# A hybrid attention and convolution block: mixer weights split in block 0 only, stored and loaded back, with layernorms on VectorE

## The reference

```
h   = LN0(concat(meta, x))
q, k, v, cb, cc, ch, gates = split(h @ w_in)          # 512,128,128,512,512,512,2048
y_attn = window_attention(q, k, v, sinks) @ w_attn_out # chunks of 64, own + previous + meta, ALiBi, sink
y_conv = (cb * conv3(cc * ch)) @ w_conv_out            # causal, 3 taps, depthwise
g_a, g_c = sigmoid(gates)
h = LN1(alpha * h + (g_a * y_attn + g_c * y_conv) @ w_o)
h = LN2(alpha * h + hierarchical_moe(h))               # 4 groups x 8 experts, top 2
```

## Time and profile before

| | |
|---|---|
| median of three runs | 4327.14 us |
| the profiled execution, its own time | 4333.28 us |
| its span, first to last instruction | 4331.5 us |
| mean granted TensorE clock | 0.988 |
| PE, weight load, DVE, ScalarE, POOL busy | 4171, 3429, 2519, 1773, 1095 us |
| DMA moved | 601 MB, mean 139 GB/s |

### The profile page before, as it was taken

One profiled execution on the slowest core, in us unless ns is written; L12 is line 12 of the kernel. 1 busy time (PEld: TensorE's weight loads), 2 busy tenths in 40 slices (PEclk: granted clock), 3 DMA queues, 4 the chain that ended last, 5 costly groups with the idle time before them and its releaser, 6 DMA issues. The chain is left out here.

```text
span 4331.5 us, 62892 instructions
## 1 busy us (share of the span) xinstructions
PE 4171.0 (96%) x20252; PEld 3428.8 (79%) x20253; DVE 2518.7 (58%) x3263; ACT 1773.0 (41%) x2950; POOL 1094.6 (25%) x1117
## 2 busy tenths in 40 slices
PE   7999999999999999999999999499999999999997
PEld 7887887887887888888888887388788888778886
DVE  5555555555555655645645645777666666765664
ACT  2422422422422422422422422466555555654553
POOL 4022032022022021121121121134333333333333
PEclk9999999999999999999999999799999999999998
DMA  6333333333333333333332332187666666765562
GB/s 171 85 107 103 93 102 98 99 104 97 102 104 89 107 106 85 107 104 89 111 102 80 117 102 78 54 289 248 246 199 198 206 199 234 251 203 198 194 204 90
DMA packets 569472, 601.49 MB, mean 139 GB/s; under 512 B 104080, under 2 KB 426640, under 8 KB 569248
## 3 DMA queue, kind: packets, MB, share of 16 engines
q1 hardware_dynamic: 521152, 476.88, 35.5%
q0 software_dynamic: 48096, 121.71, 8.4%
HBM read 527.15 MB, written 124.78 MB: 151 GB/s over the span
## 5 line engine op out<-in xcount | busy, mean ns | idle before, releaser
L826 PE MATMUL bank<-hT_hi,w_hi 128*128 128x512 f32 x2176 | 864.8, 397 | 30.1 <-DVE w_lo L658 21.3
L658 DVE TENSOR_TENSOR w_lo<-raw,w_hi 128x1024 fp32r<-128x1024 f32 x400 | 597.3, 1493 | 485.5 <-ACT w_hi L517 484.4
L827 PE MATMUL bank<-hT_lo,w_hi 128*128 128x512 f32 x2176 | 850.6, 391 | 2.4 <-issue 2.4
L828 PE MATMUL bank<-hT_hi,w_lo 128*128 128x512 f32 x2176 | 849.2, 390 | 0.0
L1565 PE MATMUL e_bank<-e_w_hi,e_xT_hi 128*128 128x512 f32 x1312 | 521.9, 398 | 14.2 <-DVE e_xT_lo L1488 12.4
L826 PEld LDWEIGHTS bank<-hT_hi,w_hi 128*128 128x128 f32 x2176 | 408.9, 188 | 140.4 <-DVE w_lo L658 32.6
L1567 PE MATMUL e_bank<-e_w_hi,e_xT_lo 128*128 128x512 f32 x1312 | 514.3, 392 | 0.0
L1566 PE MATMUL e_bank<-e_w_lo,e_xT_hi 128*128 128x512 f32 x1312 | 513.4, 391 | 0.0
L1493 DVE TENSOR_TENSOR e_w_lo<-e_raw,e_w_hi 128x1024 fp32r<-128x1024 f32 x384 | 444.4, 1219 | 117.7 <-ACT e_w_hi L1441 110.8
L828 PEld LDWEIGHTS bank<-hT_hi,w_lo 128*128 128x128 f32 x2176 | 408.9, 188 | 87.4
L827 PEld LDWEIGHTS bank<-hT_lo,w_hi 128*128 128x128 f32 x2176 | 409.3, 188 | 86.6 <-issue 5.4
(11 more groups left out here) (277 smaller groups left out, 7173.3 us busy)
## 6 DMA issues: line engine op xcount, KB each, us to landing
raw<-in_w_in_dram SPq DMA_DIRECT2D x251, 512.0 KB, 3.9
e_raw<-in_w_exp_gate_dram SPq DMA_DIRECT2D x128, 512.0 KB
e_raw<-in_w_exp_up_dram SPq DMA_DIRECT2D x128, 512.0 KB
e_raw<-in_w_exp_down_dram SPq DMA_DIRECT2D x128, 512.0 KB
h_rows<-h_rows SPq DMA_DIRECT2D x72, 512.0 KB, 3.5
raw<-in_w_o_dram SPq DMA_DIRECT2D x64, 512.0 KB, 3.8
raw<-in_w_in_dram SPq DMA_DIRECT2D x64, 256.0 KB, 3.7
raw<-in_w_attn_out_dram SPq DMA_DIRECT2D x64, 256.0 KB, 2.8
```

What stands on the lines that cost most here:

```text
L658: v.tensor_tensor(w_lo[:, s % 2, :], raw[:, s % RAW, :], w_hi[:, s % 2, :].bitcast(FP32), ALU.subtract).then_inc(lo_ready, 1)
L826: pe.matmul(out, hi, x_hi, start=first, stop=False)
L827: pe.matmul(out, hi, x_lo, start=False, stop=False)
L828: return pe.matmul(out, lo, x_hi, start=False, stop=last)
```

## The change

- **The split is done once.** Block 0 is written out ahead of the loops (`block_of_strips(0, True)`), and only there are strips loaded raw (3 buffers) and split, now two strips ahead. SP stores each split strip, hi and lo together, 1 MB, to a DRAM tensor `split_weights`. The loops run over blocks 1 to 7 and load the stored 1 MB into one of four slots: SP waits until strip s is finished on PE (`hold(sp, strip_done, ...)`), then loads strip s+3. PE waits for the load (`w_in`), ScalarE and DVE have no split there.
- **x loads** stand at MIX0 + 3 + i and no longer at MIX0 + 8 + i in SP's order.
- **Loop ends**: the loops of PE, ScalarE and DVE are written with a hint for the branch back; those of SP and POOL are as before.
- **Attention** and the v transposes go by ATT0 = CONV0 + 1, one strip later.
- **Layernorms**: DVE does both passes, subtract and gain, then scale and bias; POOL keeps the reciprocal deviation.
- DVE waits for its own mT_lo of the strip before, ahead of overwriting work[2], and the branch on block 0 for bias_prev becomes straight code.

The diff, cut to its core:

```diff
-    RAW = 5
-    assert N % RAW == 0 and N % 2 == 0
+    RAW, META_RAW = 3, 5
+    SLOTS = 4
+    ahead = RAW
+    slot_of = list(range(SLOTS)) * 5 + [0, 1, 2] + list(range(SLOTS)) * 6 + [0, 1, 2]
+    def first_slot(s):
+        return (s + 1) % RAW
     CONV0 = 2 + PAIRS
+    ATT0 = CONV0 + 1
...
-        raw = sb("raw", [P, RAW, D])
-        w_hi = sb("w_hi", [P, 2, D], F32R)
-        w_lo = sb("w_lo", [P, 2, D], F32R)
+        split_d = nc.dram_tensor("split_weights", [N, P, 2 * D], FP32).ap()
...
+        slots = [place(at, f"w_slot{i}", [P, 2, D], F32R) for i in range(SLOTS)]
+        raw = place([weights + 4 * 6 * D], "raw", [P, RAW, D])
...
-        X_AT = {MIX0 + 8 + i: i for i in range(TILES)}
+        X_AT = {MIX0 + 3 + i: i for i in range(TILES)}
...
             def _(sp):
-                def load(s, b):
-                    hold(sp, lo_ready, b * N + s + 1)
-                    for dst, src in strip_dmas(*strips[s % N], raw[:, s % RAW, :]):
+                def load_raw(s):
+                    if s >= RAW:
+                        sp.wait_ge(lo_ready, s - RAW + 1)
+                    for dst, src in strip_dmas(*strips[s], raw[:, s % RAW, :]):
                         sp.dma_start(dst, src).then_inc(raw_in[s % RAW], 16)
+                def store_split(s):
+                    sp.wait_ge(lo_ready, s + 1)
+                    sp.dma_start(split_d[s], slots[first_slot(s)][:, :, :].rearrange("p h d -> p (h d)").bitcast(FP32))\
+                      .then_inc(w_out[first_slot(s)], 16)
+                def load_split(s, b):
+                    sp.wait_ge(w_out[first_slot(s)], 16 * (sum(first_slot(q) == first_slot(s) for q in range(s + 1))))
+                    sp.dma_start(slots[slot_of[s]][:, :, :].rearrange("p h d -> p (h d)").bitcast(FP32), split_d[s])\
+                      .then_inc(w_in[slot_of[s]], 16)
+                def block_of_loads(b, first):
                     for s in range(N):
-                        load(s + 1, b)
+                        if first:
+                            store_split(s)
+                        if first and s + ahead < N:
+                            load_raw(s + ahead)
+                        else:
+                            hold(sp, strip_done, b * N + s + 3)
...
+                            load_split((s + ahead) % N, b + (s + ahead) // N)
...
             def _(po):
...
-                        scale(b * LNS + i1 - 1, i1 - 1, h, g1, b1)
-                    scale(b * LNS + TILES - 1, TILES - 1, h, g1, b1)
...
             def _(a):
-                def split_hi(b, s):
-                    uses = raw_uses(s, b) if s < N else raw_uses(0, b + 1)
-                    a.wait_ge(raw_in[s % RAW], uses)
-                    a.wait_ge(strip_done, b * N + s + 1)
-                    a.activation(w_hi[:, s % 2, :], raw[:, s % RAW, :], ACT.Copy).then_inc(hi_ready, 1)
+                def split_hi(s):
+                    a.wait_ge(raw_in[s % RAW], raw_uses(s))
+                    if s >= RAW:
+                        a.wait_ge(strip_done, s - RAW + 3)
+                        a.wait_ge(w_out[first_slot(s)], 16 * (sum(first_slot(q) == first_slot(s) for q in range(s))))
+                    a.activation(slots[first_slot(s)][:, 0, :], raw[:, s % RAW, :], ACT.Copy).then_inc(hi_ready, 1)
...
-                        split_hi(b, s + 1)
+                        if first and s + 2 < N:
+                            split_hi(s + 2)
...
+                block_of_strips(0, True)
+                with nc.Fori(1, BLOCKS, engines=bass.OrderedEngineSet([a.engine]), hint_back_edge=True) as b:
+                    block_of_strips(b, False)
...
             def _(v):
...
-                    v.tensor_scalar(rows[:, i1, :], rows[:, i1, :], moments[:, i1, 0:1], rstd[:, i1, 0:1],
-                                    ALU.subtract, ALU.mult).then_inc(ln_normed, 1)
+                    gain, shift = (g1, b1) if rows is h else (g0, b0)
+                    v.scalar_tensor_tensor(out=rows[:, i1, :], in0=rows[:, i1, :], scalar=moments[:, i1, 0:1],
+                                           in1=gain[:, :], op0=ALU.subtract, op1=ALU.mult).then_inc(ln_normed, 1)
+                    v.wait_ge(ln_normed, n + 1)
+                    v.scalar_tensor_tensor(out=rows[:, i1, :], in0=rows[:, i1, :], scalar=rstd[:, i1, 0:1],
+                                           in1=shift[:, :], op0=ALU.mult, op1=ALU.add).then_inc(ln_done, 1)
...
-                        split_lo(s + 1)
+                        if first and s + 2 < N:
+                            split_lo(s + 2)
...
             def _(pe):
...
-                        n = s - CONV0
-                        if s == CONV0:
-                            taken = out_no[(s - 1, 0)]
+                        n = s - ATT0
+                        if s == ATT0:
+                            taken = out_no[(CONV0 - 1, 0)]
...
-                        pe.wait_ge(lo_ready, b * N + RAW + s + 1)
+                        if first:
+                            pe.wait_ge(lo_ready, s + 1)
+                            w_of = slots[first_slot(s)]
+                        else:
+                            pe.wait_ge(w_in[slot_of[s]], w_uses(s, b))
+                            w_of = slots[slot_of[s]]
```

More of the change, by code:

```diff
@@ L245, in _ @@
                 sp.dma_start(xs[:, :, :], x[0:TOK, :].rearrange("(t p) d -> p t d", p=P)).then_inc(x_in, 16)
-                for n in range(1, RAW):
+                for n in range(1, META_RAW):
                     load_strip(n)
@@ L402, in mixer @@
         h1_out = [sem(f"h1_out{i}") for i in range(TILES)]
+        w_in = [sem(f"w_in{i}") for i in range(SLOTS)]
+        w_out = [sem(f"w_out{i}") for i in range(RAW)]
         hi_ready = sem("hi_ready")
@@ L439, in mixer, with raw_uses, w_uses @@
         LNS = 2 * TILES
[L441 to L446, removed]
+        def raw_uses(s):
+            return sum(16 * len(strip_dmas(*strips[q], raw[:, 0, :])) for q in range(s % RAW, s + 1, RAW))
+        def w_uses(s, b):
+            slot = slot_of[s]
+            return 16 * ((b - 1) * slot_of.count(slot) + slot_of[0:s + 1].count(slot))
         with nc.Block() as block:
@@ L473, in _ @@
                             sp.dma_start(xs[:, i1, :], x[bass.ds(nxt * TOK + i1 * P, P), :]).then_inc(x_in[i1], 16)
+                for s in range(ahead):
+                    load_raw(s)
+                block_of_loads(0, True)
+                with sp.Fori(1, BLOCKS) as b:
+                    block_of_loads(b, False)
+                for s in range(ahead):
+                    sp.wait_ge(w_in[slot_of[s]], w_uses(s, BLOCKS))
                 for i1 in range(TILES):
@@ L643, in _, with split_lo, block_of_strips @@
                 v.sem_inc(hx_lo, 1)
[L644 to L647 removed]
+                def split_lo(s):
+                    slot = slots[first_slot(s)]
+                    v.wait_ge(hi_ready, s + 1)
+                    v.tensor_tensor(slot[:, 1, :], raw[:, s % RAW, :], slot[:, 0, :].bitcast(FP32),
+                                    ALU.subtract).then_inc(lo_ready, 1)
+                def block_of_strips(b, first):
                     steps = [0]
@@ L724, in _ @@
                              .then_inc(s_prep, 1)
-                            if n == 1:
-                                with v.If(b == 0):
-                                    v.tensor_copy(bias[0:CHUNK, :, META:PREV], bias_prev[:, :, :])\
-                                     .then_inc(prev_set, 1)
+                            if n == 1 and first:
+                                v.tensor_copy(bias[0:CHUNK, :, META:PREV], bias_prev[:, :, :]).then_inc(prev_set, 1)
                                 v.wait_ge(prev_set, 1)
@@ L802, in _ @@
                     assert steps[0] == DVE_STEPS
+                for s in range(2):
+                    split_lo(s)
+                block_of_strips(0, True)
+                with nc.Fori(1, BLOCKS, engines=bass.OrderedEngineSet([v.engine]), hint_back_edge=True) as b:
+                    block_of_strips(b, False)
                 v.wait_ge(wo_taken, BLOCKS * 2 * TILES + 1)
```

72 lines of the change are left out of this document (34 added, 38 removed).

## The result

The changed kernel takes 4297.57 us (median of 7 runs, 4289.16 to 4307.51) against 4331.25 us for the kernel before (7 runs, 4320.51 to 4341.16). The ratio is 0.9923, 95% interval 0.9905 to 0.9941: 33.7 us faster by the medians. The forecast was 4295 and 32 us. Its profiled execution took 4303.45 us, with a span of 4301.6; the one of the kernel before took 4333.28.

What follows compares the result with a forecast made beforehand. TensorE, busy 96% of the span, was taken as the bound, so only its waits could pay. Waits of 25.5 us plus loop ends of 7, less 1 for block 0, about 32, took 4327.1 to 4295 us; range 4285 to 4305.

Steps and rivals of the forecast that it cites:

- What bounds: Whole kernel: TensorE busy 96% of the span, so only its waits, all in strips 0 to 7 of a block, can pay.
- The split leaves: 1.21 + 1.28 us a block: PE's waits for VectorE's split before strip 5 (1.21 us) and behind the second scores in strip 7 (1.28 us) go.
- Attention later: 0.69: At the v transposes behind the last q strip, PE's 0.69 us wait for ScalarE's q copy goes in each block.
- Loop ends: 1.0, bounds 0.4 to 1.4: At block starts, stops for issue behind the branch shrink: 1.0 us each, 7 us over 7 ends, bounds 3 to 10.
- strip 1's part: At a block's start, PE's 0.56 us wait for the late split of strip 1 goes, even if the hint does nothing.
- Layernorms at nothing, cover named: VectorE pays 10 to 13 us a block more, hidden before the router (strip 18) and strip 41; uncovered, at most 13.
- Loads, 0 to 3 us a block: Stored 1 MB loads land in 6.5 us of 10.9, slack 4.4; h1 stores in strips 4 to 7 fit; cost 0.
- Block 0: Raw loads plus 1 MB stores fit at DMA share 0.84: cost 0, bounds 0 to 40 us; 1 us deducted for attention.
- A: Strips with h1 stores in seven loop blocks: queue waits replace the split's, 4313 to 4322 us, no change; 14%.
- B: Strips 4 to 8 of loop blocks, and block 0: queue too slow at 230 GB/s, 4366 to 4405 us, slower; 10%.
- D: Loop blocks: PE's split waits become equally long waits for weights; only q copy and loop ends won, 4315 us; 4%.
- C: Product pitch falls 1 ns or small waits inside attention go: 10 to 15 us more gain, 4280 to 4285 us; 14%.

Runs made afterwards that it cites:

- w_only: Kernel before with only the stored weights and their x loads: 4312.3 us, ratio 0.9949, block period 325.1 against 328.4.
- a_att_early: Changed kernel with v transposes and attention back at their earlier strip: block period 323.5 against 322.6, 4312.4 us in one execution.
- b_hint: Kernel before with only the hint on the loops of PE, ScalarE and VectorE: block period 326.6 against 328.4, 4334.2 us in one execution.
- a_pool_ln: Changed kernel with the layernorms' gain and bias passes back on POOL: block period 322.6, unchanged; 4304.1 us in one execution.
- b_ln: Kernel before with only the layernorms changed, both passes on VectorE: block period 331.6 against 328.4, 4357.5 us in one execution.
- a_extra: Changed kernel with one more unused 512 KB load a strip in blocks 1 to 7: block period 322.6, unchanged; 4293.6 us in one execution.
- a_ahead2: Changed kernel with stored weights loaded for strip s+2 and not s+3: block period 325.8 against 322.6, 4333.7 us in one execution.
- b_all: Kernel before with later attention, VectorE layernorms and hint, weights still split in every block: 4367.3 us, ratio 1.0081.
- b_att: Kernel before with only attention and v transposes one strip later: block period 331.3 against 328.4, 4356.4 us in one execution.

## Why the prediction was right, point by point

- **What bounds.** Right in the main. Nothing in the mixing strips moved (144.9 us from strip 18 to strip 42 before, 144.95 after), and of the 5.8 us by which the period fell all but some 0.7 come from the places named in strips 0 to 7. The rest came from strips 5 to 14, in pieces too small to be in the list of waits.
- **The split leaves: 1.21 + 1.28 us a block.** Shown by w_only: 1.21 and 1.35, and 0.5 more in strips 5, 13 and 14. The whole period fell by 3.3.
- **Attention later: 0.69.** It was 0.95 (a_att_early). The bracket is idle time against a modelled end; from start to start it was 1.08 - 0.23 = 0.85, and I should have used that, as I did for strip 5.
- **Loop ends: 1.0, bounds 0.4 to 1.4.** The mis-sized term: 1.8 for the hint alone, 1.9 in the changed kernel. It failed in the sentence "a block has one in full or both in part". The seven block starts of the kernel before cost PE 1.5 to 1.9 us each against b_hint's, at three places and not two, and the trace of before had them all. The next step failed as well, that strip 1's part "goes whatever the hint does": in w_only it went, and PE's own stop took its place, 1.3 to 1.9 us a block start. So had the hint done nothing, the loop ends would have given about 0 us and not 3. The rule of the Trainium skill that the prediction named ("Runtime: NRT & Kernel Launch", Instruction fetch mechanics), that a branch to code outside the window is a fetch stall, agrees with these stops, and in the loop blocks of the changed kernel, with the hint, none is left.
- **Layernorms at nothing, cover named.** Right for this kernel: 0.00 (a_pool_ln). But the price "if that cover were gone", at most 13 us a block, was worked out as busy time. With the split behind them the same passes cost 3.2 us a block net (b_ln: the four waits of 1.23 and small ones behind them cost 5.4, and strips 4 to 6 gave 2.2 back), and that figure comes from the order on DVE, which busy time doesn't tell.
- **Loads, 0 to 3 us a block.** Right at 0, and too careful: 1 MB landed in 4.8 us (median) and not 6.5, in a queue where the h1 stores went from 3.5 to 7.9 us without anybody waiting.
- **Block 0.** Forecast 2.2 us shorter than before; it was 4.5, at a DMA share of 0.79 (0.84 forecast). Strips 2 to 17 alone gave 4.1, as much as in the loop blocks: the small waits went here too, and the 1 us that the prediction kept back for attention beside a split wasn't paid.
- **What I missed.** Block 1's wait for a store (4.0 us) and the longer router part (5.0 us, 3.8 of them the stop). I walked the stored weights through a steady block and never through the seam between block 0 and the loop, nor through the loop's exit. Six blocks gained 5.7 each for 4.2 forecast, 9 us more in all, and block 0 gave 2.3 more; block 1 gave 2.4 less and the router part took 5.0 back. So 32 against 33.7 is partly luck: errors of opposite sign, and the experts' spread of over 20 us lies on the whole time besides.
- **Rivals.** A, B and D are refuted by the changed kernel's own trace, which has one wait for the stored weights in all its loop blocks, in block 1, and by a_extra and a_ahead2. C (smaller waits elsewhere, or a lower pitch) is half there: the pitch stayed, but small waits inside attention did go, 0.5 us a block, a third of what C asked or less.

Open: what makes PE stop for 3.8 us behind the last block. It needs the hint, it isn't the hint alone, and it isn't the three useless loads in the queue. DVE's stop of 3.69 us at the same loop exit in a_pool_ln, where only POOL's and DVE's code was edited, suggests that it depends on how the code lies; no run here varies that by itself. Open too is why the clock falls behind one wait of 2.3 us and not behind the next.

## What to carry to other kernels

Price a moved operation by what is queued behind it on its engine, not by the engine's busy share: VectorE was under 60% busy, and two passes of 1.28 us in front of a split cost PE 3 us a block net. Before a preparation step is taken off a loop, its neighbours must be costed with and without it: layernorm and attention edits lost 0.8% by themselves with the hint and were free or a gain once the split was gone. And walk a change through the seams (first block into loop, loop into what follows), where a slot, a store or a stop for issue is met once and nothing stands ahead to hide it. And add up small losses from start to start over the whole stretch: a list of waits leaves out the smallest of them, as at the block's start here.

## What the runs showed of the hardware

- Behind a branch back over a long loop body DVE stood for issue in two stops, 31.5 us in seven block starts (4.5 each), in the kernel before, and in one stop, 37.9 us in six (6.3 each), in the changed kernel without the hint. The DMA share was 0.35 and 0.51 there, but the code differs as well, and no run separates the two. With the hint on the loop these stops were gone in both kernels, and a block was 1.8 to 1.9 us shorter.
- 263 GB/s of DMA traffic for a whole block, 326 over 30 us, left the pitch of PE's products (0.227 us) and the period unchanged.
- Stores of 1 MB landed in 5.1 us in the median, but one issued right behind a 1 MB load was waited for until 10 us after its issue.
- After 2.08 us of idle PE the granted clock stood at 0.72 over the next 6 us, and that cost 1.8 us on top of the wait. After idle PE of 2.33 to 2.37 us it fell in 7 of 16 cases (b_all, b_att), after 1.94 and after 1.4 us it didn't.
